# A decoder layer step on one core: key and value units of the paged cache set in pairs between weight chunks

## The reference, cut to what matters

```python
def sample_attention(q, k, v, iq, ik, iw, pos, cache_k, cache_v, cache_idx_k, page_table, topk):
...
    score = index_scores(iq, iw, ik_all)
    score = jnp.where(key_pos[None, None, :] <= pos[None, :, None], score, -jnp.inf)
    _, idx = lax.top_k(score, topk)
...
    return sparse_attend(q.astype(k_sel.dtype), k_sel, v_sel, valid)
```

## Time and profile before

| | |
|---|---|
| median of 3 runs | 1351.96 us |
| profiled execution | 1351.73 us |
| its span, first to last instruction | 1350.1 us |
| mean granted clock | 0.992 |
| PE busy | 1307.5 us (97%) |
| DVE, ACT, POOL busy | 767.4, 597.8, 172.9 us |
| DMA | 271.5 MB, mean 201 GB/s |
| first and last key unit | 126.9 and 270.6 us |
| first and last value unit | 290.1 and 402.1 us |

### The profile page before, as it was taken

How to read it: one execution, slowest core, us unless ns; L and a number is a source line. 1 busy time by engine, 2 the same in 40 slices (tenths; PEclk the granted TensorE clock), 3 DMA queues, 4 the chain that set the end, 5 groups by cost and what they waited for, 6 DMA issues and landing times.

```text
span 1350.1 us, 25403 instructions
## 1 busy us (share of the span) xinstructions
PE 1307.5 (97%) x9748; PEld 1214.4 (90%) x9748; DVE 767.4 (57%) x1261; ACT 597.8 (44%) x964; POOL 172.9 (13%) x293
## 2 busy tenths in 40 slices
PE   9889999999999999999999999999999999999995
PEld 8868777776659899999999999999999999999994
DVE  5556877784436576556656655655655545443434
ACT  5243322343333476455445546445545433333434
POOL 5520000022220041001100100100100500000002
PEclk9989999999999999999999999999999999999998
DMA  8668799978986545655555655555555655555552
GB/s 269 188 191 298 235 355 372 324 279 318 348 321 217 153 130 166 174 170 157 171 162 155 176 165 156 173 171 158 163 168 170 184 167 160 161 164 158 170 156 71
DMA packets 98124, 271.50 MB, mean 201 GB/s; under 512 B 13097, under 2 KB 20338, under 8 KB 97874
## 3 DMA queue, kind: packets, MB, share of 16 engines
q1 hardware_dynamic: 89650, 249.84, 59.4%
q0 software_dynamic: 7808, 19.54, 4.1%
q10 hardware_dynamic: 544, 0.50, 0.1%
HBM read 264.66 MB, written 5.18 MB: 200 GB/s over the span
## 4 chain that ended last, share of the span: by engine, by line
PE 83%; SPq 5%; DVE 4%; DMA 3%; issue 3%; ACT 1%; POOLq 0%; ACTq 0%; DVEq 0%; POOL 0%
PE G L466 26%; PE G L467 25%; PE G L468 25%; SPq L292 2%; PE A L799 2%; SPq L286 1%; DMA raw<-in_w_in 1%; PE A L614 1%; DMA raw<-in_w_iq 1%; DVE w_lo L1393 1%; SPq L307 1%; DMA raw<-in_w_out 1%; SPq L359 1%; DMA v_ring_x<-in_v_cache 1%; ACT w_hi L1048 1%
## 5 line engine op out<-in xcount | busy, mean ns | idle before, releaser
L1393 DVE TENSOR_TENSOR w_lo<-raw,w_hi 128x1024 fp32r<-128x1024 f32 x354 | 435.3, 1230 | 441.1 <-ACT w_hi L1048 440.2
L1048 ACT ACTIVATE w_hi<-raw 128x1024 fp32r<-128x1024 f32 x354 | 373.9, 1056 | 551.2 <-PE G L468 444.0
L466 PE MATMUL G<-x_hi,w_hi 128*128 128x290 f32 (+1 forms) x1856 | 558.9, 301 | 14.5 <-DVE w_lo L1393 6.9
L467 PE MATMUL G<-x_lo,w_hi 128*128 128x290 f32 (+1 forms) x1856 | 552.8, 298 | 0.0
L468 PE MATMUL G<-x_hi,w_lo 128*128 128x290 f32 (+1 forms) x1856 | 549.6, 296 | 0.0
L466 PEld LDWEIGHTS G<-x_hi,w_hi 128*128 128x128 f32 x1856 | 350.1, 189 | 23.9 <-issue 14.6
L467 PEld LDWEIGHTS G<-x_lo,w_hi 128*128 128x128 f32 x1856 | 351.9, 190 | 0.2
L468 PEld LDWEIGHTS G<-x_hi,w_lo 128*128 128x128 f32 x1856 | 349.6, 188 | 0.0
L466 PE MATMUL G<-h_hi,w_hi 128*128 128x288 f32 x704 | 208.9, 297 | 0.0
L467 PE MATMUL G<-h_lo,w_hi 128*128 128x288 f32 x704 | 207.7, 295 | 0.0
L468 PE MATMUL G<-h_hi,w_lo 128*128 128x288 f32 x704 | 207.1, 294 | 0.0
(11 more groups left out here) (298 smaller groups left out, 1134.5 us busy)
## 6 DMA issues: line engine op xcount, KB each, us to landing
raw<-in_w_up SPq DMA_DIRECT2D x176, 512.0 KB, 3.6
raw<-in_w_down SPq DMA_DIRECT2D x88, 512.0 KB, 3.6
k_ring<-in_kT_cache SPq DMA_DIRECT2D x128, 256.0 KB, 4.2
raw<-in_w_in SPq DMA_DIRECT2D x48, 512.0 KB, 5.6
raw<-in_w_out SPq DMA_DIRECT2D x32, 512.0 KB, 6.5
v_ring_x<-in_v_cache POOLq DMA_DIRECT2D x44, 256.0 KB, 6.3
v_ring_p<-in_v_cache SPq DMA_DIRECT2D x32, 256.0 KB, 4.8
v_ring_x<-in_v_cache SPq DMA_DIRECT2D x28, 256.0 KB, 4.1
```

The source lines that it names most:

```text
L466: pe.matmul(out, hi, xh, start=start, stop=False)
L467: pe.matmul(out, hi, xl, start=False, stop=False)
L1048: act.activation(w_hi[:, c, 0:width], raw[:, c, 0:width], ACT.Copy).then_inc(hi_done, 1)
L1393: dve.tensor_tensor(w_lo[:, c, 0:width], raw[:, c, 0:width], w_hi[:, c, 0:width].bitcast(f32), ALU.subtract).then_inc(lo_done, 1)
```

## The change

The tables that place the units are rewritten. The order of the chunks, of the units among themselves and of everything else stays. Key units stand two after each of chunks 4, 6, 8, 9, 11, 12, 14, 16, 17, 19, 20, 22, 24, 25, 27 and 29. Value units 8 to 31 stand two in each of slots 0, 2, 3, 6, 8, 9, 12, 14, 15, 18, 20 and 21.

```diff
-FILL = {0: (63, (8,)), 1: (None, (9,)), 2: (64, (10,)), 3: (None, (11,)), 4: (None, (12,)), 5: (None, (13,)),
-        6: (65, (14,)), 7: (None, (15,)), 8: (66, (16,)), 9: (None, (17,)), 10: (None, (18,)), 11: (67, (19,)),
-        12: (68, (20,)), 13: (None, (21,)), 14: (69, (22,)), 15: (None, (23,)), 16: (None, (24,)), 17: (None, (25,)),
-        18: (70, (26,)), 19: (None, (27,)), 20: (71, (28,)), 21: (None, (29, 30)), 22: (None, (31,)), 23: (None, ())}
+FILL = {0: (63, (8, 9)), 1: (None, ()), 2: (64, (10, 11)), 3: (None, (12, 13)), 4: (None, ()), 5: (None, ()),
+        6: (65, (14, 15)), 7: (None, ()), 8: (66, (16, 17)), 9: (None, (18, 19)), 10: (None, ()), 11: (67, ()),
+        12: (68, (20, 21)), 13: (None, ()), 14: (69, (22, 23)), 15: (None, (24, 25)), 16: (None, ()), 17: (None, ()),
+        18: (70, (26, 27)), 19: (None, ()), 20: (71, (28, 29)), 21: (None, (30, 31)), 22: (None, ()), 23: (None, ())}
...
 def units_after(i):
 
-    twice = (9, 12, 15, 18, 21, 25)
-    if i < 3 or i == 7 or i > 29:
+    pairs = (4, 6, 8, 9, 11, 12, 14, 16, 17, 19, 20, 22, 24, 25, 27, 29)
+    if i not in pairs:
         return range(0)
-    first = i - 3 - (i > 7) + sum(d < i for d in twice)
-    return range(first, first + 1 + (i in twice))
+    first = 2 * pairs.index(i)
+    return range(first, first + 2)
```

## The result

The changed kernel takes **1387.3 us** (median of 4 executions, 1383.93 to 1389.51) where the kernel before takes 1351.68 beside it: a ratio of 1.0251, 95% interval 1.0214 to 1.0289. The forecast was 1362.0 with a range of 1350.5 to 1366. The direction was right; the loss is 35.6 us instead of 10.3, outside the range.

What follows compares the result with a forecast made beforehand. In the key stretch PE is the bound by a hair, with the chain SP, DMA, ACT, DVE, PE right behind. Terms +8.9, -0.15 and +1.6 sum to +10.3 on 1351.7, giving 1362 us; range 1350.5 to 1366.

Steps and rivals of the forecast that it cites:

- Boundaries 8 to 20: Key units: page loads of adjacent pairs fill SP's queue, weight chunks land late and PE waits; decisive term, +7.6 us.
- 8.56 and 9.79: Key part: us from pair start to chunk issue, and from there to the end total three boundaries on.
- The rival that the DMA engines set the stretch: Key stretch: same bytes at 97% busy, so waits and savings meet near 1351 to 1354 us; chance 0.08.
- Up to boundary 8: First key units: unit 0 no longer runs in a wait, boundary 6 pays for a pair; +1.3 us.
- From boundary 20: Late key units: 12 units in 6 groups save 0.75 us, DVE's mask additions cost 0.6; together -0.15 us.
- Value waits on POOL: Value part: odd units loaded by POOL land late at four places, 0 to 4 us each, 0.5 taken; +2.0 us.
- The two waits for the low halves: Value part: prompt scores after the first and third pair of heads wait 1.33 us each; +2.7 us.
- The softmax and `o_sb` waits: Value part: existing PE waits go, -0.85 us at the first transpose, -0.96 at the last unit and gather.
- the last unit's 0.25: End of the value part: an existing 0.25 us wait that goes, part of the -0.96 us.
- The merges: Fewer unit groups save mode switches: up to 0.33 us each among keys, -1.3 us in sum for values.
- the 0.14 each: Saving taken per merge where another narrow product keeps the switch, bounded by 0 and 0.33 us; nine for the values.
- Full clock nearly throughout: Whole kernel before: granted clock read as full nearly throughout; no time was charged for a lower clock.

Runs made afterwards that it cites:

- POOL's help: Changed kernel with the odd key units from 9 on loaded by POOL instead of SP: 1376.33 us (1.0187).
- The run with busy products: Changed kernel with products whose result nobody uses issued ahead of its longest waits, so that TensorE doesn't idle: 1380.08 us (1.0208).
- the evenly spaced run: Kernel before with value units in pairs in every second slot, 0 to 22, keys as before: 1352.67 us (1.0009).
- either cure: Changed kernel with odd key units from 9 on loaded by POOL, 1376.33 us, or with the second unit's pages behind the next chunk, 1374.33 us.

## Why the prediction was wrong

**Boundaries 8 to 20: right.** +7.6 was forecast, +8.6 came; the sum of queue and landing placed the totals of 11, 12, 15, 19 and of chunk 20 within 1.0 us. Moving pages behind the chunk (about half of what it gained in the profiled execution arises in this part) shows that the order of SP's queue is a cause. The argument that 8.56 and 9.79 explain the wait at boundary 12 to 0.1 us was no evidence, as both were read off that very wait; the five totals after are the evidence. The rival that the DMA engines set the stretch is excluded as the whole cause, their share fell to 91%, but they may limit any cure: with POOL's help the chunks land in 9.4 us.

**Up to boundary 8: +1.3 forecast, +3.0 found.** The wait at the total of boundary 3 grew to 2.57 us, as unit 0 no longer runs ahead of it, and behind it 130 to 140 us have a granted clock of 0.83, a loss of 1.7 us, as much as the difference. The run with busy products settles it: there 130 to 140 us is at full clock, and from the total of boundary 3 to the product that waits for `k_t` PE takes 25.0 us, where the changed kernel takes 26.5 and the kernel before 23.7. Without the clock the loss is the 1.3 that was forecast.

**From boundary 20: -0.15 forecast, +7.4 found.** Of the waits, this is the first step that failed. I let the delay end with the middle total of chunk 20 and charged 0.6 us for DVE's additions. But chunks stay late behind each pair, and DVE, in its order, makes `w_lo` first and then the addition that PE's next mask product waits for:

```profile
251.83 1.23 DVE L1393 TENSOR_TENSOR w_lo<-raw,w_hi 128x1024 fp32r<-128x1024 f32 x1 [4.26 <-ACT w_hi L1048]
252.97 0.68 DVE L1565 CUSTOM_DVE_ANT_0 s_all<-A,s_all 128x512 f32<-128x512 f32 x1
```
```profile
253.72 0.77 PE L622 MATMUL A<-mask,spread 32*128 32x512 f32 x1 [1.91 <-DVE stat L1565]
```

It comes twice, 1.91 and 2.38 us (at 253.72 and 282.71). With the 0.5 us more on `m_lo` these are 4.8; the lower clock behind the 5.70 us wait and at 250 us is at most 5.1 more.

**Value waits on POOL: +2.0 forecast, +7.4 found.** The four places were named right (units 13, 19, 25 and 31: 1.60, 1.40, 1.51 and 2.54 us, with 0.17 and 0.46 at the units ahead); the size was not. I gave 0.5 within bounds of 0 to 4, since the median landing of the earlier trace rows just fitted. The load behind a pair isn't a median load: SP issues the four pages of unit 12 from 344.44 and a chunk at 346.39, POOL those of unit 13 from 345.71 to 347.4, and these took 7.4 us. The two waits for the low halves were 2 x 1.31, as worked out. The softmax and `o_sb` waits went as forecast, but the last unit's 0.25 became 2.54.

**The merges: right and small.** 1.3 us for the values, by the evenly spaced run; the 0.14 each behind it was a choice between 0 and 0.33, so the agreement is partly luck. For the keys the saving is not separable from the waits.

**The term that was missing: the clock.** "Full clock nearly throughout" was read as a property of the kernel; it held while no wait was over 1.57 us (120 to 460 us); behind a wait of 2.02 us at 478.63 even the kernel before falls to 0.88 in 480 to 490 us. The prediction put this term at nothing, and it is the largest that failed. In the value part 17.7 us are made of 8.3 us of waits, less 1.3 for the merges, and 10.7 that no wait explains; the loss by the granted clock is 13.7 there, and keeping TensorE busy gave back 6.9. By difference over the whole kernel: 36.7 us less 23.5 of new waits, plus 1.3 for the value merges, leave some 14.5 us for the clock, and a little more by what the key merges saved. The Trainium skill, "TensorE: Matmul & The Clock Gate", HAM oscillation, says that a kernel which works in short stretches between DMA waits begins each stretch at the lower clock and pays for that every time. The waits of its case are longer than any that I forecast but the one in chunk 20, so by it only that wait term would have needed a second one behind it. The trace agrees there (0.50 in 230 to 235 us), and goes further: the other windows at 0.50 quoted above stand behind waits of 1.3 to 2.5 us.

**The rivals.** The worst case, 1366 to 1371, named "POOL's loads land in 8 us or more before all four adjacent pairs, and the queue term is 11", with a chance of 0.09. Its first half nearly came, and even that case was 16 us short, since none of the cases had a price for the clock.

Settled by runs: the order of the queue, the places of the value pairs, and that the lower clock costs time of its own. Open: what decides whether the clock falls behind a wait, with which the value part of one placement moved between 96 and 104 us, and why chunk 20 still waits 3.9 to 4.5 us with either cure; competing transfers are what the landing times suggest, no run separates them.

## What to carry to other kernels

On an engine that is 97% busy at full clock, price a new wait twice: its own length, and the stretch at 1.2 GHz that may follow it. A range for the time should cover both cases, since the same wait had it behind it in one kernel and not in another. And compare the granted clocks before a gain is put down to an edit: of the gain between the profiled executions by the queue's order, half arose where the edit changes nothing. Grouping work that releases buffers also groups the loads behind it: a queue that was just full stands idle and then holds back whatever is queued behind the burst, so put the urgent load between the two halves of the burst. Spacing the groups evenly cured the values but not the keys, whose queue was full already. A median landing time is not the price of loads that leave together.

## What the runs showed of the hardware that I had not expected

- An idle time of 0.95 us was followed by a window at a granted clock of 0.72, one of 0.65 us by a window at 0.51, and one of 0.29 us by a window at 0.62. The same waits of 0.29 and 0.65 us in the run with evenly spaced values had full clock behind them, and so had 1.95 us in the changed kernel, so the wait's length alone doesn't decide it.
- More work can take less time: 86 products of no use made the changed kernel 7.2 us faster.
- With the same placement of key units up to boundary 20, the middle total of chunk 20 stood at 221.47, 223.62, 224.16, 221.81, 223.39, 221.23 and 222.22 us in seven kernels' profiled executions. Of this spread of 2.9 us, 2.3 are there at the total of boundary 3 already (128.38 to 130.63). The wait for the late chunk, which I had read as a fixed 1.35 us, was between 1.35 and 2.32.
